# RWKV-7 chunk steps of a decoder trunk: zero-padded whole-array matmuls, another order of outputs and side work

## The chip, the cores and the metric

The kernel runs on one core of one Trainium2 chip. The metric is the device time of one execution in microseconds, the median of several runs. The profile comes from one further execution of the same program.

## The reference, cut to what matters

The program computes two layers of a hybrid trunk for 256 tokens of 1024 channels in float32: a gated mixer of three branches (RG-LRU, gated DeltaNet, RWKV-7), then a PEER expert layer. The change lies in the phase that computes the RWKV branch and, beside it, the input projections of other branches ("side" projections). The recurrence of that branch is, for 16 heads of 64 channels:

```python
def step(state, inp):
    r_t, w_t, k_t, v_t, kk_t, kka_t = inp
    s_kk = einsum('bhvk,bhk->bhv', state, kk_t)
    state = state * w_t[:, :, None, :] - s_kk[..., None] * kka_t[:, :, None, :] + v_t[..., None] * k_t[:, :, None, :]
    return state, einsum('bhvk,bhk->bhv', state, r_t)
...
o = (o - mean) * rsqrt(var + eps)            # group norm over the 64 channels of a head
o = o * lnx_w + lnx_b
o = (o + bonus) * gate
```

## The kernel before

**Phase and loop.** `rwkv_phase` runs once per layer. It walks over eight channel tiles of 128 channels (two heads each): seven in a hardware loop (`more=True`) and the last one outside it (`more=False`). Each engine has its own body: `pe_body` (TensorE), `act_body` (ScalarE), `vec_body` (VectorE), `pool_body` (GpSimd). The engines run their own lists in order and meet at semaphores: `te.wait_ge(V.sem, V.at("S0", i))` waits until VectorE has passed the point labelled "S0" of tile i. The order of the work is written by hand; nothing plans it.

**One tile.** The 256 tokens are four chunks of 64. q counts the chunks; b = q // 2 is the block of 128 tokens, hf = q % 2 the half of the 128 partitions in which the chunk's tokens lie. A tile's work is:
- transposes (`bkT`, `vT`) of NBt, KH and the value, then the small products `g0`, `g1` (L915) that give the masked matrices G1, G2 within a chunk;
- T0 (L926), AV and `bonus` (L937, L940);
- the inversion of 64x64 unit triangular matrices in five levels (`invert64_pe`, L495) into TT;
- the four chunk steps, below;
- the group norm on VectorE (L1217 to L1231), the output transpose `yT` (L982), and y (L1233 to L1237).

**A chunk step before.** St is the 128x128 state of the two heads. R (L955) is the product of the chunk's keys with St, 64 output rows; VectorE adds AVO to it (L1188). U (L963) multiplies by TT; ScalarE copies it to Um (L1070). L968 adds the queries' product with St into the output bank b3. L973 and L974 are the state's increment from the value Vt and from Um, over the 64 rows of the chunk; VectorE masks it (t1, L1201) and updates St (L1204, or L1206 for q = 0), for which SP = decayed St was made at L1190. L976 adds the output's part within the chunk (`O`), and VectorE adds bank b3 to O (L1209).

**Side work.** While TensorE waits in this chain it works on other products: `pe_piece` is part of the projection of r, k, v of the next tile (12 parts, in the inversion's `fill`), and `pe_side` parts of the five side projections f0 to f4 (20 parts). These use split float32: a weight tile and x are each a high part (rounded) and a rest, so a single k (128 of the 1024 inputs) is three matmuls of 128x128 by 256 columns (L332 to L334, L808 to L810). A part is two k. The high parts of the weights are made on ScalarE (`act_round`, L315, L829), the rests on VectorE (`vec_rest`, L320) for r, k, v, f2, f3, f4, and on GpSimd (L834) for f0 and f1. `act_side` copies a finished side projection out. `turn` (L291) is a matmul of the identity whose result nobody reads.

**What VectorE does for the next tile.** `vec_sums`, `vec_roots` (two half reciprocals, L768), `vec_keys` (L772 to L777), `vec_ends` (KH and the chunk ends, L780, L781), `vec_queries` (L785, L786), `vec_bonus` (L763) and `vec_piece` (L871) stand between the steps' own operations. `pe_sums` (L723) is the matmul that sums squares.

**Loads.** SyncE issues the weight tiles in the order r, k, v, `rwkv_up`, f0 to f4 of each tile, each behind the release of its slot in the ring.

Of the kernel before, what the change touches and what calls it, by code (L numbers as in the profile page):

```python
# [99 lines left out]
def _program(nc, ctx, A, out, book):  # L100
# [199 lines left out]
    class Split:  # L300
# [25 lines left out]
        def project(self, te, ps, n, parity, part, x_parts=x_parts):  # L326
            if part % 2 == 0:
                te.wait_ge(self.low, 2 * n + part // 2 + 1)
            for k in range(2 * part, 2 * part + 2):
                w_hi, w_lo = (f32r(w_parts[:, x, parity, k * P:(k + 1) * P]) for x in range(2))  # L330
                x_hi, x_lo = (f32r(x_parts[:, x, k]) for x in range(2))
                te.matmul(ps, w_hi, x_hi, start=(k == 0), stop=False)  # L332
                te.matmul(ps, w_hi, x_lo, start=False, stop=False)  # L333
                mm = te.matmul(ps, w_lo, x_hi, start=False, stop=(k == KT - 1))  # L334
            if part % 2:
                mm.then_inc(self.used, 1)
# [260 lines left out]
    def rwkv_phase(l):  # L597
# [20 lines left out]
        side_rounded, side_rest = lsem("rw_side_rounded"), lsem("rw_side_rest")  # L618

# [20 lines left out]
        Vt = r_(NB, P)  # L640
# [4 lines left out]
        Rs, Um, St, SP, t1 = r_(P), r_(P), r_(P), r_(P), r_(P)  # L645
# [11 lines left out]
        O4 = O.rearrange("p b (h c) -> p (b h) c", h=2)  # L657

# [3 lines left out]
        with nc.Block() as block:  # L662
# [107 lines left out]
            def vec_keys(v, i):  # L770
                v.wait_ge(VA.sem, VA.now(i))
                v.tensor_tensor(kk, kkr, rs, ALU.mult).then_inc(VA.sem, VA.one())  # L772
                v.wait_ge(VA.sem, VA.now(i))
                v.scalar_tensor_tensor(nb, kk, -1.0, aa, ALU.mult, ALU.mult).then_inc(VA.sem, VA.one())
                v.wait_ge(VA.sem, VA.now(i))
                v.wait_ge(SA.sem, SA.at("Pi", i))
                v.tensor_tensor(NBt, nb, Pi, ALU.mult).then_inc(VA.sem, VA.one())  # L777
# [10 lines left out]
            def pe_side(te, i, js, more):  # L788
                for j in js:
                    n, part = divmod(j, 4)  # L790
                    if part == 0:
# [10 lines left out]
                    if n < 2:  # L802
                        if part % 2 == 0:
                            te.wait_ge(side_rest, 4 * i + 2 * n + part // 2 + 1)
                        for k in range(2 * part, 2 * part + 2):
                            w_hi, w_lo = f32r(side_high[:, n, k * P:(k + 1) * P]), f32r(side_low[:, n, k * P:(k + 1) * P])
                            x_hi, x_lo = (f32r(x_parts[:, x, k]) for x in range(2))
                            te.matmul(f_bank[n], w_hi, x_hi, start=(k == 0), stop=False)  # L808
                            te.matmul(f_bank[n], w_hi, x_lo, start=False, stop=False)
                            mm = te.matmul(f_bank[n], w_lo, x_hi, start=False, stop=(k == KT - 1))  # L810
                        if part == 3:
                            mm.then_inc(EF.sem, EF.one(f"f{n}"))
                    else:
                        W.project(te, f_bank[n], tile(f"f{n}", i), parity(f"f{n}"), part)
# [60 lines left out]
            def pe_body(te, i, more):  # L875
                def fill(lev, y):
# [3 lines left out]
                    if more and (lev, y) == (5, 0):  # L880
                        pe_sums(te, i + 1)
                    if more:
                        pe_piece(te, i + 1, 2 * lev + y)
                    elif lev and (y == 0 or lev == 5):
                        if lev == 1:
                            te.wait_ge(SF.sem, SF.at("f0", i))
                        turn(te, ps_in[0], 2)

                def side(*js):
                    pe_side(te, i, js, more)  # L890

# [5 lines left out]
                side(0)  # L897
                te.wait_ge(VA.sem, VA.at("KH", i))
                for x, src in enumerate((NBt, KH)):
                    for b in range(NB):  # L900
                        mm = te.transpose(b5[:, (2 * x + b) * P:(2 * x + b + 1) * P], src[:, b * P:(b + 1) * P], ident)
                mm.then_inc(E.sem, E.one("bkT"))
# [1808 lines left out]
```

## Time and profile before

| | us |
|---|---|
| median of 3 runs | 3372.75 |
| lowest, highest | 3370.45, 3377.39 |
| span of the profiled execution, and its own time | 3373.3 |
| busy: TensorE, VectorE, ScalarE, GpSimd | 3242.0, 2293.5, 1747.5, 251.9 |
| first RWKV phase, last tile's y ends | 455.3 |
| second RWKV phase, last tile's y ends | 2131.2 |

The profiled execution's first to last instruction is its span; nothing beyond the span is recorded. A row of a timeline gives the start in us, the time in us, the engine, the line, the operation, output <- inputs and the count; in brackets stands the engine's idle time just before it and what released it. "issue" there is a wait for nothing that the profile shows. TensorE's matmuls are pipelined, so the busy time of one (some 0.28 us) is longer than the distance to the next start; distances between starts are what matters. An fp32 matmul appears as two records, so "x4" for such lines is two matmuls; transposes and the split products (fp32r) appear as one.

### The profile page before, as it was taken

The numbers are of one execution on the slowest core, as the hardware profiler recorded it, in microseconds if no ns is written. First come the engines' busy times: TensorE is split into PE (matmuls) and PEld (weight loads), VectorE is DVE, ScalarE is ACT, GpSimd is POOL, SyncE is SP. The second block draws the span as 40 slices with busy tenths as digits, with TensorE's granted clock in tenths as the row PEclk, the third lists the DMA queues.
The fourth block names the chain that finished last, engine by engine and source line by source line (L and its number), as shares of the span: only waits on it lengthen the run. The fifth ranks groups of instructions, "written<-read, shape, count | busy, mean of one in ns | idle before, by whom it ended". The sixth has DMA issues, their size and how long they took to land. (4 is left out here: it accounts for less than half of the span.)

```text
span 3373.3 us, 74285 instructions
## 1 busy us (share of the span) xinstructions
PE 3242.0 (96%) x24946; PEld 2825.3 (84%) x24946; DVE 2293.5 (68%) x5014; ACT 1747.5 (52%) x3657; POOL 251.9 (7%) x238
## 2 busy tenths in 40 slices
PE   8999999999999999999989999999999999999998
PEld 7878788889998788888778778888898978888886
DVE  5666666655886677777666665666558866777776
ACT  5555454433296555555555554544323965555554
POOL 2212101100000000000022111021000000000000
PEclk9999999999999999999999999999999999999999
DMA  3222322223323555555432222232242245555553
GB/s 135 91 80 74 112 73 101 92 81 145 106 81 131 187 187 188 191 190 190 158 114 70 96 70 104 76 106 81 82 177 86 75 146 188 189 187 187 190 190 130
DMA packets 122236, 433.34 MB, mean 128 GB/s; under 512 B 15744, under 2 KB 18048, under 8 KB 121344
## 3 DMA queue, kind: packets, MB, share of 16 engines
q1 hardware_dynamic: 122112, 431.74, 36.1%
q8 instruction: 71, 1.16, 0.1%
q14 instruction: 53, 0.43, 0.0%
HBM read 430.64 MB, written 1.05 MB: 128 GB/s over the span
## 5 line engine op out<-in xcount | busy, mean ns | idle before, releaser
L2360 PE MATMUL bank<-x_both,u_parts 128*128 128x512 f32 x1536 | 557.8, 397 | 1.8 <-DVE u_parts L2480 1.8
L2344 PE MATMUL bank<-v_parts,act_high 128*128 128x512 f32 x1024 | 405.0, 396 | 5.9 <-DVE v_parts L2485 4.7
L2346 PE MATMUL bank<-v_parts,act_low 128*128 128x512 f32 x1024 | 399.9, 391 | 0.0
L2356 PE MATMUL bank<-x_both,u_parts 128*128 128x256 f32 x1536 | 399.5, 281 | 0.0
L2345 PE MATMUL bank<-v_parts,act_high 128*128 128x512 f32 x1024 | 398.8, 389 | 0.0
L332 PE MATMUL bank<-x_parts,w_parts 128*128 128x256 f32 x1248 | 394.4, 316 | 1.5 <-DVE w_parts L320 1.5
L2480 DVE TENSOR_TENSOR u_parts<-u_raw,u_parts 128x512 fp32r<-128x512 f32 x384 | 265.5, 692 | 191.7 <-ACT u_parts L2415 191.6
L333 PE MATMUL bank<-x_parts,w_parts 128*128 128x256 f32 x1248 | 352.6, 283 | 0.0
L334 PE MATMUL bank<-x_parts,w_parts 128*128 128x256 f32 x1248 | 351.7, 282 | 0.0
L2485 DVE TENSOR_TENSOR v_parts<-v_raw,v_parts 128x512 fp32r<-128x512 f32 x512 | 329.7, 685 | 31.6 <-ACT v_parts L2422 28.3
L2360 PEld LDWEIGHTS bank<-x_both,u_parts 128*128 128x128 f32 x1536 | 288.5, 188 | 62.5 <-issue 2.6
L2415 ACT ACTIVATE u_parts<-u_raw 128x512 fp32r<-128x512 f32 x384 | 242.5, 632 | 187.5 <-PE bank L2360 147.3
L2422 ACT ACTIVATE v_parts<-v_raw 128x512 fp32r<-128x512 f32 x512 | 292.1, 618 | 27.4 <-DMA v_raw<-in_v 22.7
L2356 PEld LDWEIGHTS bank<-x_both,u_parts 128*128 128x128 f32 x1536 | 289.7, 189 | 16.3
L320 DVE TENSOR_TENSOR w_parts<-ring,w_parts 128x512 fp32r<-128x512 f32 x344 | 254.3, 776 | 27.3 <-ACT w_parts L315 26.5
L332 PEld LDWEIGHTS bank<-x_parts,w_parts 128*128 128x128 f32 x1248 | 237.1, 190 | 40.0 <-issue 19.6
L333 PEld LDWEIGHTS bank<-x_parts,w_parts 128*128 128x128 f32 x1248 | 238.4, 191 | 0.9
L334 PEld LDWEIGHTS bank<-x_parts,w_parts 128*128 128x128 f32 x1248 | 238.1, 191 | 0.0
L2344 PEld LDWEIGHTS bank<-v_parts,act_high 128*128 128x128 f32 x1024 | 193.0, 188 | 52.6 <-DVE v_parts L2485 16.5
L2453 ACT ACTIVATE slots<-slots 128x256 f32<-128x256 f32 x192 | 80.7, 420 | 296.0 <-DVE slots L2531 296.0
L2346 PEld LDWEIGHTS bank<-v_parts,act_low 128*128 128x128 f32 x1024 | 192.2, 188 | 43.3
L2345 PEld LDWEIGHTS bank<-v_parts,act_high 128*128 128x128 f32 x1024 | 192.4, 188 | 39.8
(374 smaller groups left out, 6334.4 us busy)
## 6 DMA issues: line engine op xcount, KB each, us to landing
v_raw<-in_v SPq DMA_DIRECT2D x256, 512.0 KB, 3.5
u_raw<-in_u SPq DMA_DIRECT2D x192, 512.0 KB, 4.5
ring<-in_w_side SPq DMA_DIRECT2D x80, 512.0 KB, 3.5
ring<-in_w_gdn SPq DMA_DIRECT2D x64, 512.0 KB, 3.5
ring<-in_w_rwkv SPq DMA_DIRECT2D x48, 512.0 KB, 6.1
ring<-in_w_gdn_side SPq DMA_DIRECT2D x32, 512.0 KB, 3.5
ring<-in_u SPq DMA_DIRECT2D x32, 512.0 KB, 3.6
u_ring<-in_u SPq DMA_DIRECT2D x32, 512.0 KB, 3.5
```

The costliest lines, as they stand in the source:

```text
L320: v.tensor_tensor(f32r(w_parts[:, 1, parity, self.cols(half)]), raw[:, self.cols(half)], w_parts[:, 0, parity, self.cols(half)], ALU.subtr ...
L332: te.matmul(ps, w_hi, x_hi, start=(k == 0), stop=False)
L333: te.matmul(ps, w_hi, x_lo, start=False, stop=False)
L334: mm = te.matmul(ps, w_lo, x_hi, start=False, stop=(k == KT - 1))
L2344: te.matmul(ps, f32r(w_hi), f32r(x_hi), start=start, stop=False, **kw)
L2345: te.matmul(ps, f32r(w_hi), f32r(x_lo), start=False, stop=False, **kw)
L2346: return te.matmul(ps, f32r(w_lo), f32r(x_hi), start=False, stop=stop, **kw)
L2356: return te.matmul(banks[r % 4][:, T:2 * T], f32r(u_lo[:, cols]), f32r(xhigh[:, k]), start=False, stop=stop)
L2360: mm = te.matmul(banks[r % 4][:, :].rearrange("p (x t) -> p x t", x=2), f32r(u_hi[:, cols]), f32r(x_both[:, :, k]), start=(k == 0), stop=( ...
L2422: a_.activation(f32r(v_hi[r % 2][:, half(n)]), v_raw[:, r % 2, half(n)], ACT.Copy).then_inc(v_high, 1)
L2480: v.tensor_tensor(f32r(u_lo[:, half(n)]), u_raw[:, r % 2, half(n)], u_hi[:, half(n)], ALU.subtract).then_inc(u_low, 1)
L2485: v.tensor_tensor(f32r(v_lo[r % 2][:, half(n)]), v_raw[:, r % 2, half(n)], v_hi[r % 2][:, half(n)], ALU.subtract)\
```

## The change

- **Whole array.** Vt becomes VX, with two copies for the chunk halves, each zero in the other half's 64 rows; Um becomes UX likewise. The zeros are written once per phase on GpSimd. With them the state's increment runs over all 128 rows, R and the queries' product fill all 128 output rows, and only U and the reads within the chunk (`reads`) stay 64x64.
- **Outputs beside the next step's U.** The queries' product follows R at once; the reads of step q-1 stand behind U of step q. The outputs alternate between two banks (OB = b3, b4). ScalarE's copy of U no longer waits for O. VectorE's output add of step q-1 (`out_add`) stands behind the R-add of step q and side pieces.
- **Side projections by single k.** The 20 parts become 40 k: 2 and 14 ahead of T0, then 1 behind R, 1 behind U, 2 behind the state's increment, and the rest at the end.
- **Order on VectorE.** SP is made behind the state update; f3's rest goes from q=1 to q=2, f4's stays in q=3, behind an output add; `vec_roots`, `vec_bonus`, `vec_piece`, the keys, KH and the queries move as the diff shows.
- **Others.** `pe_sums` goes behind the piece of its level; the side copy of f3 goes behind the root on ScalarE; `idle` puts two turns before a wait in the last tile.
- The prologue (tile 0) calls the same VectorE functions, with the first root half ahead of the last shift.

```diff
-Vt = r_(NB, P)
+VX = r_(2, NB, P)
...
-Rs, Um, St, SP, t1 = r_(P), r_(P), r_(P), r_(P), r_(P)
+Rs, St, SP, t1 = r_(P), r_(P), r_(P), r_(P)
+UX = r_(2, P)
...
+OB = (b3, b4)
...
-def vec_keys(v, i):
+def vec_key(v, i):
...
+def vec_beta(v, i):
...
+def vec_betas(v, i):
...
-    v.tensor_tensor(NBt, nb, Pi, ALU.mult).then_inc(VA.sem, VA.one())
+    v.tensor_tensor(NBt, nb, Pi, ALU.mult).then_inc(VA.sem, VA.one("NBt"))
...
-        if part == 3:
+        if k == KT - 1:
-        W.project(te, f_bank[n], tile(f"f{n}", i), parity(f"f{n}"), part)
+        W.project_k(te, f_bank[n], tile(f"f{n}", i), parity(f"f{n}"), k)
...
         pe_gates(te, i + 1)
-    if more and (lev, y) == (5, 0):
-        pe_sums(te, i + 1)
     if more:
...
         turn(te, ps_in[0], 2)
+    if more and (lev, y) == (5, 0):
+        pe_sums(te, i + 1)
...
+def idle(n):
+    if not more:
+        turn(te, b6, n)
...
 rows = lambda q: slice(64 * q, 64 * q + 64)
-side(0)
-te.wait_ge(VA.sem, VA.at("KH", i))
-for x, src in enumerate((NBt, KH)):
-    for b in range(NB):
-        mm = te.transpose(b5[:, (2 * x + b) * P:(2 * x + b + 1) * P], src[:, b * P:(b + 1) * P], ident)
-mm.then_inc(E.sem, E.one("bkT"))
+te.wait_ge(VA.sem, VA.at("NBt", i))
+for b in range(NB):
+    te.transpose(b5[:, b * P:(b + 1) * P], NBt[:, b * P:(b + 1) * P], ident)
 for b in range(NB):
...
 te.matmul(b6[:, T:2 * T], small[:, P:2 * P], SG, start=True, stop=True).then_inc(E.sem, E.one("gate"))
+te.wait_ge(VA.sem, VA.at("KH", i))
+for b in range(NB):
+    mm = te.transpose(b5[:, (2 + b) * P:(3 + b) * P], KH[:, b * P:(b + 1) * P], ident)
+mm.then_inc(E.sem, E.one("bkT"))
+side(0, 1)
...
-side(1, 2, 3, 4)
+side(*range(2, 16))
...
-                               G2[rows(hf), 2 * hh + b, x], Vt[rows(hf), b, hh * HD:(hh + 1) * HD], start=True, stop=True)
+                               G2[rows(hf), 2 * hh + b, x], VX[rows(hf), hf, b, hh * HD:(hh + 1) * HD], start=True, stop=True)
...
+def reads(q):
+    b, hf = divmod(q, 2)
+    for hh in range(2):
+        mm = te.matmul(OB[hf][rows(hf), hh * HD:(hh + 1) * HD], G1[rows(hf), 2 * hh + b, 1], UX[rows(hf), hf, hh * HD:(hh + 1) * HD],
+                       start=(q == 0), stop=True, skip_group_check=True)
+    mm.then_inc(E.sem, E.one(f"O{q}"))
+left = list(range(16, 40))
+step_side = lambda n: side(*(left.pop(0) for _ in range(n)))
 for q in range(T // CH):
...
     if q:
-        if not more:
-            turn(te, b4, 1)
+        idle(2)
         te.wait_ge(V.sem, V.at(f"S{q - 1}", i))
...
             te.wait_ge(SA.sem, SA.at("a", i + 1))
-        te.matmul(b5[rows(hf), 0:P], KR[:, b, 0, rows(hf)], St, start=True, stop=True).then_inc(E.sem, E.one(f"R{q}"))
-        side(2 * q + 7)
-        if not more:
-            turn(te, b4, 1)
+        te.matmul(b5[:, 0:P], KR[:, b, 0], St, start=True, stop=True).then_inc(E.sem, E.one(f"R{q}"))
+        if q > 1:
+            te.wait_ge(V.sem, V.at(f"o{q - 2}", i))
+        te.matmul(OB[hf][:, 0:P], KR[:, b, 1], St, start=True, stop=False, skip_group_check=True)
+        step_side(1)
         te.wait_ge(V.sem, V.at(f"R{q}", i))
...
     if q:
-        te.wait_ge(V.sem, V.at(f"o{q - 1}", i))
-        te.matmul(b3[rows(hf), 0:P], KR[:, b, 1, rows(hf)], St, start=True, stop=False)
-    side(2 * q + 8)
+        reads(q - 1)
+    if q < 3:
+        te.matmul(b2[:, 0:P], BK[:, 2 + b], VX[:, hf, b], start=True, stop=False)
+    step_side(1)
     te.wait_ge(S.sem, S.at(f"U{q}", i))
-    te.sem_inc(passed, 1)
     if q < 3:
-        te.matmul(b2[:, 0:P], BK[rows(hf), 2 + b], Vt[rows(hf), b], start=True, stop=False)
-        te.matmul(b2[:, 0:P], BK[rows(hf), b], Um[rows(hf)], start=False, stop=True).then_inc(E.sem, E.one(f"S{q}"))
-    for hh in range(2):
-        mm = te.matmul(b3[rows(hf), hh * HD:(hh + 1) * HD], G1[rows(hf), 2 * hh + b, 1], Um[rows(hf), hh * HD:(hh + 1) * HD],
-                       start=(q == 0), stop=(hh == 1) or q == 0)
-    mm.then_inc(E.sem, E.one(f"O{q}"))
-side(15, 16, 17, 18, 19)
+        te.matmul(b2[:, 0:P], BK[:, b], UX[:, hf], start=False, stop=True).then_inc(E.sem, E.one(f"S{q}"))
+        step_side(2)
+    else:
+        te.sem_inc(passed, 1)
+        reads(q)
+side(*left)
 te.wait_ge(V.sem, V.at("on", i))
...
-a.activation(Vt, vps, ACT.Copy).then_inc(S.sem, S.one("Vt"))
+for hf, rows in enumerate(halves):
+    a.activation(VX[rows, hf], vps[rows], ACT.Copy).then_inc(S.sem, S.one(f"V{hf}"))
...
     a.wait_ge(E.sem, E.at(f"U{q}", i))
-    if q:
-        a.wait_ge(E.sem, E.at(f"O{q - 1}", i))
     rows = halves[q % 2]
-    a.activation(Um[rows], b7[rows, 0:P], ACT.Copy).then_inc(S.sem, S.one(f"U{q}"))
+    a.activation(UX[rows, q % 2], b7[rows, 0:P], ACT.Copy).then_inc(S.sem, S.one(f"U{q}"))
     if q == 0 and more:
...
         act_round(a, i, "f4")
-act_side(a, i, 3)
...
 a.activation(va4, va4, ACT.Sqrt).then_inc(S.sem, S.one("sd"))
+act_side(a, i, 3)
 a.wait_ge(SF.sem, SF.at("f2", i))
...
         vec_sums(v, i + 1)
+    if n == 2 and not more:
+        W.skip(v, W.low, tile("r", NI), 3)
     if n == 5:
-        if not more:
-            W.skip(v, W.low, tile("r", NI), 3)
         vec_rest(v, i, "f2")
     if more and n == 5:
-        vec_bonus(v, i + 1)
+        vec_roots(v, i + 1, 0)
...
+def out_add(q):
+    b, hf = divmod(q, 2)
+    rows = halves[hf]
+    v.wait_ge(E.sem, E.at(f"O{q}", i))
+    v.wait_ge(S.sem, S.at("AVO", i))
+    v.tensor_tensor(O[rows, b], O[rows, b], OB[hf][rows, 0:P], ALU.add).then_inc(V.sem, V.one(f"o{q}"))
...
         v.tensor_tensor(Rs[rows], b5[rows, 0:P], AVO[rows, b], ALU.add).then_inc(V.sem, V.one(f"R{q}"))
-        if q < 3:
-            v.tensor_scalar(SP, St, end, None, ALU.mult).then_inc(V.sem, V.one())
-        if q != 2:
-            vec_rest(v, i, {1: "f3", 3: "f4"}[q])
-        if q < 3 and more:
-            vec_roots(v, i + 1, q - 1)
+        if q == 1 and more:
+            vec_piece(v, i + 1, 2)
+            vec_bonus(v, i + 1)
+        if q == 2:
+            vec_rest(v, i, "f3")
         if q == 2 and more:
-            vec_keys(v, i + 1)
+            vec_roots(v, i + 1, 1)
         if q == 3 and more:
-            vec_ends(v, i + 1)
+            vec_key(v, i + 1)
+            vec_beta(v, i + 1)
+        out_add(q - 1)
+        if q == 3:
+            vec_rest(v, i, "f4")
     if q < 3:
...
-    v.wait_ge(E.sem, E.at(f"O{q}", i))
-    v.wait_ge(S.sem, S.at("AVO", i))
-    v.tensor_tensor(O[rows, b], O[rows, b], b3[rows, 0:P], ALU.add).then_inc(V.sem, V.one(f"o{q}"))
-    if q == 0 and more:
-        vec_piece(v, i + 1, 2)
...
-if more:
-    vec_queries(v, i + 1)
+        if q < 2:
+            v.wait_ge(V.sem, V.now(i))
+            v.tensor_scalar(SP, St, ends[:, q + 1:q + 2], None, ALU.mult).then_inc(V.sem, V.one())
+out_add(3)
...
 v.tensor_scalar(va4, va4, 1.0 / HD, GN_EPS, ALU.mult, ALU.add).then_inc(V.sem, V.one("var"))
+if more:
+    vec_betas(v, i + 1)
 v.wait_ge(S.sem, S.at("sd", i))
...
 v.tensor_tensor(O4, O4, bc(va4), ALU.mult).then_inc(V.sem, V.one("on"))
+if more:
+    vec_ends(v, i + 1)
+    vec_queries(v, i + 1)
 v.wait_ge(E.sem, E.at("yT", i))
...
+norm.all_ready(g)
+for n, x in enumerate((VX, UX)):
+    for hf in range(2):
+        if n + hf:
+            g.wait_ge(zeros, 2 * n + hf)
+        g.memset(x[halves[1 - hf], hf], 0.0).then_inc(zeros, 1)
+g.wait_ge(zeros, 4)
```

## Rows read from the trace of the kernel before

**Rows 1.** The page, busy time, share and instructions per engine.
```profile
PE 3242.0 (96%) x24946; PEld 2825.3 (84%) x24946; DVE 2293.5 (68%) x5014; ACT 1747.5 (52%) x3657; POOL 251.9 (7%) x238
```
**Rows 2.** TensorE's timeline, three output transposes; then a windows row (PEclk is the clock).
```profile
148.10 0.44 PE L982 MATMUL bank<-made_of_shapes,arena 128*128 128x128 f32 x2 [1.36 <-DVE arena L1231]
...
199.84 0.44 PE L982 MATMUL bank<-made_of_shapes,arena 128*128 128x128 f32 x2 [1.35 <-DVE arena L1231]
...
253.23 0.44 PE L982 MATMUL bank<-made_of_shapes,arena 128*128 128x128 f32 x2 [1.36 <-DVE arena L1231]
...
202.00:203.00 1.00, 1.00 (x6) 0.85 (x4) 0.13 (x1) 0.99 (x2) 0.00 (x0) 0.50 0.03 12
```
**Rows 3.** Waits of TensorE, 98 to 409 us: total, times, longest.
```profile
PE bank L955 <- DVE arena L1204: 4.8, 12, 0.4
PE bank L723 <- DVE arena L756: 4.2, 6, 0.7
```
**Rows 4.** TensorE's timeline, U of q=0, then the step q=2.
```profile
179.88 0.44 PE L963 MATMUL bank<-arena 64*64 64x64 f32 x4
...
186.96 0.43 PE L955 MATMUL bank<-arena 128*64 128x128 f32 x2 [0.40 <-DVE arena L1204]
187.32 0.39 PE L332 MATMUL bank<-x_parts,w_parts 128*128 128x256 f32 x1
...
188.23 0.44 PE L963 MATMUL bank<-arena 64*64 64x64 f32 x4
188.60 0.43 PE L968 MATMUL bank<-arena 128*64 128x128 f32 x2
...
189.87 0.49 PE L973 MATMUL bank<-arena 64*128 64x128 f32 x2
...
191.35 0.43 PE L955 MATMUL bank<-arena 128*64 128x128 f32 x2 [0.40 <-DVE arena L1204]
```
**Rows 5.** TensorE's timeline in the last tile: a side matmul, then turns.
```profile
447.10 0.28 PE L334 MATMUL bank<-x_parts,w_parts 128*128 128x256 f32 x1
447.22 0.38 PE L291 MATMUL bank<-made_of_shapes 128*128 128x128 f32 x2
...
453.64 1.28 PE L291 MATMUL bank<-made_of_shapes 128*128 128x128 f32 x10
```
**Rows 6.** VectorE's timeline in the steps.
```profile
184.88 0.95 DVE L768 RECIPROCAL arena<-arena 128x128 f32<-128x128 f32 x1
...
187.43 0.28 DVE L1188 TENSOR_TENSOR arena<-bank,arena 64x128 f32<-64x128 f32 x1 [0.20 <-PE bank L955]
...
190.61 0.29 DVE L1201 TENSOR_TENSOR arena<-bank,made_of_shapes 128x128 f32<-128x128 f32 x1 [0.38 <-PE bank L974]
190.94 0.35 DVE L1204 SCALAR_TENSOR_TENSOR arena<-arena 128x128 f32<-128x128 f32 x1
...
192.14 1.29 DVE L320 TENSOR_TENSOR w_parts<-ring,w_parts 128x512 fp32r<-128x512 f32 x2
```
**Rows 7.** ScalarE's timeline, the copy of U.
```profile
188.78 0.27 ACT L1070 ACTIVATE arena<-bank 64x128 f32<-64x128 f32 x1 [4.12 <-PE bank L963]
```
**Rows 8.** VectorE's timeline in the tail.
```profile
194.73 0.29 DVE L1209 TENSOR_TENSOR arena<-arena,bank 64x128 f32<-64x128 f32 x1 [0.88 <-PE bank L976]
195.06 0.43 DVE L785 TENSOR_TENSOR arena<-arena 128x256 f32<-128x256 f32 x1
...
199.15 0.18 DVE L1229 RECIPROCAL arena<-arena 128x4 f32<-128x4 f32 x1 [1.22 <-ACT arena L1082]
```
**Rows 9.** SyncE's issues of r, k, v; their landings; ScalarE ahead of the r round.
```profile
194.71 1.57 SPq L584 DMA_DIRECT2D ring<-in_w_rwkv  x3
...
DMA to landing us min/median/max: 4.8/6.1/6.7
...
201.23 1.28 ACT L315 ACT_TABLE_LOAD   x1
```
**Rows 10.** GpSimd's timeline in the first prologue.
```profile
25.14 3.04 POOL L834 TENSOR_TENSOR side_low<-ring,side_high 128x512 fp32r<-128x512 f32 x2 [3.83 <-ACT side_high L829]
```

More of the change, by code:

```diff
@@ L326, in project, with project_k @@
         def project(self, te, ps, n, parity, part, x_parts=x_parts):
-            if part % 2 == 0:
-                te.wait_ge(self.low, 2 * n + part // 2 + 1)
             for k in range(2 * part, 2 * part + 2):
[L330 to L335, printed above, removed]
+                self.project_k(te, ps, n, parity, k, x_parts)
+        def project_k(self, te, ps, n, parity, k, x_parts=x_parts):
+            if k % (KT // 2) == 0:
+                te.wait_ge(self.low, 2 * n + k // (KT // 2) + 1)
+            w_hi, w_lo = (f32r(w_parts[:, x, parity, k * P:(k + 1) * P]) for x in range(2))
+            x_hi, x_lo = (f32r(x_parts[:, x, k]) for x in range(2))
+            te.matmul(ps, w_hi, x_hi, start=(k == 0), stop=False)
+            te.matmul(ps, w_hi, x_lo, start=False, stop=False)
+            mm = te.matmul(ps, w_lo, x_hi, start=False, stop=(k == KT - 1))
+            if k % (KT // 2) == KT // 2 - 1:
                 mm.then_inc(self.used, 1)
@@ L618, in rwkv_phase @@
         side_rounded, side_rest = lsem("rw_side_rounded"), lsem("rw_side_rest")
+        zeros = lsem("rw_zeros")
         number = {"r": 0, "k": 1, "v": 2, "f2": 9, "f3": 10, "f4": 11}
@@ L789, in pe_side @@
                 for j in js:
-                    n, part = divmod(j, 4)
-                    if part == 0:
+                    n, k = divmod(j, KT)
+                    if k == 0:
                         if n == 0:
@@ L802, in pe_side @@
                     if n < 2:
[L803 to L810, printed above, removed]
-                        if part == 3:
+                        if k % (KT // 2) == 0:
+                            te.wait_ge(side_rest, 4 * i + 2 * n + k // (KT // 2) + 1)
+                        w_hi, w_lo = f32r(side_high[:, n, k * P:(k + 1) * P]), f32r(side_low[:, n, k * P:(k + 1) * P])
+                        x_hi, x_lo = (f32r(x_parts[:, x, k]) for x in range(2))
+                        te.matmul(f_bank[n], w_hi, x_hi, start=(k == 0), stop=False)
+                        te.matmul(f_bank[n], w_hi, x_lo, start=False, stop=False)
+                        mm = te.matmul(f_bank[n], w_lo, x_hi, start=False, stop=(k == KT - 1))
+                        if k == KT - 1:
                             mm.then_inc(EF.sem, EF.one(f"f{n}"))
                     else:
-                        W.project(te, f_bank[n], tile(f"f{n}", i), parity(f"f{n}"), part)
+                        W.project_k(te, f_bank[n], tile(f"f{n}", i), parity(f"f{n}"), k)
             def act_round(a, i, *whats, halves=(0, 1)):
@@ L927, in pe_body @@
                 mm.then_inc(E.sem, E.one("T0"))
-                side(5, 6, 7)
                 te.wait_ge(S.sem, S.at("gate", i))
@@ L1015, in _ @@
                 W.skip(te, W.used, 3, 3, W.PRIME)
+                te.wait_ge(zeros, 4)
                 EA.end()
@@ L1276, in _ @@
                 vec_sums(v, 0)
+                vec_roots(v, 0, 0)
+                vec_piece(v, 0, 2)
                 vec_bonus(v, 0)
-                vec_piece(v, 0, 2)
-                for half in range(2):
-                    vec_roots(v, 0, half)
-                vec_keys(v, 0)
+                vec_roots(v, 0, 1)
+                vec_key(v, 0)
+                vec_beta(v, 0)
+                vec_betas(v, 0)
                 vec_ends(v, 0)
```

## The prediction

> **What bounds the kernel now.** I read the page's busy shares first: TensorE is busy 3242.0 of 3373.3 us, VectorE 68% [rows 1]. So only what shortens TensorE's own sequence, or its few gaps, moves the end. The printed chain of waits covers just the last 17 us, so I went by TensorE's timeline in the phase that the diff touches. That phase runs 16 times (8 channel tiles, two layers), 14 of them in the loop form (`more`) and two as the last tile. From one output transpose (L982) to the next is 51.74 us (148.10 to 199.84), once 53.39 (199.84 to 253.23) [rows 2]. The table of waits over six iterations shows TensorE idle before L955 (twelve times 0.40) and before L723 (six times 0.70) [rows 3]; before L982 it is 1.36 each time [rows 2]. With a third, shorter wait at L955 that is some 3.2 us of an iteration, the rest is streaming. A gain above that must come out of the matmuls' own spacing.
>
> Rows 4 show one chunk step on TensorE, R2 (the L955 of q=2) at 186.96 to R3 at 191.35: 4.39 us. R takes 0.36 to the next start, a side part of six matmuls 0.91, U 0.37, L968 0.36, again 0.91 with its edges, the two L973/L974 0.32 each, the reads 0.44, then 0.40 idle. Side matmuls in a run start 0.12 apart [rows 5], so six are 0.71 and entering and leaving them costs 0.2.
>
> **What a change of shape costs.** The edge behind a side group costs 0.1 where a 64-row block follows, but in rows 5 the full 128x128 turn L291 starts 0.12 behind the side matmul before it (447.10 to 447.22), which is the side matmuls' own spacing; and the U behind this turn comes 0.32 later, where a turn inside a run of five costs (1.28-0.27)/4.5 = 0.225. So leaving 128x128 costs about 0.1, and staying costs nothing. The old step changes the array's shape seven times (128x64, 128x128, 64x64, 128x64, 128x128, 64x128, 64x64, 128x64); the new one goes to 64x64 for U and the reads and back: twice.
> The Trainium skill says the same in "TensorEngine Tiling (Array Packing)", Key Properties: changing the tiling mode drains the engine. It gives no price. The same page speaks against the change too: with contract dimensions of 64, row tiling gives up to twice the throughput. By that rule the zero-padded whole-array matmuls would waste half; here the blocks concerned stand alone and the old K=64 pair has 0.32 per matmul [rows 4], so the trace bears out the first rule and not the second.
>
> **The steps, new.** I price a whole-array fp32 matmul of 128 columns at 0.225 [rows 5]. Its upper end is what the part-array forms cost now, 0.32 to 0.36 [rows 4]; its lower end is not below 0.2, since the same number of columns streams. A single k is three matmuls, 0.36; entry from fp32 0.1; each change of shape 0.1 to 0.15.
> - R to U: R 0.225 plus 0.1 of start-up where it waited, output half (L968's work moved here) 0.225, entry 0.1, one k 0.36, change 0.1: 1.07. The wait hidden: VectorE starts the R-add 0.47 behind R and needs 0.28 [rows 4, 6], so U could start at 0.82. Covered. (Before: 1.27.)
> - U to the second S matmul: U and the reads of the step before, eight 64x64 records: four cost 0.37 with 0.16 of edge, so eight 0.58; change 0.1; the V matmul 0.225; entry 0.1; one k 0.36: about 1.35. The U copy on ScalarE ends 0.82 behind U [rows 4, 7]: covered, also now that it no longer waits for O. (Before: 1.96.)
> - Second S matmul to the next R: the tail is VectorE's. From L974 (0.32 behind L973, so 190.19) to t1 0.42, t1 and the state update end 1.10, R at 1.16 [rows 4, 6]. TensorE's work there is 0.225 + 0.1 + two k 0.71 = 1.04, so about 0.1 idle is left of the 0.40.
> The step from R1 to R2 is 3.6 (was 4.39). R2 to R3 is set by VectorE: behind the R-add (to 0.75) stand the f3 rest, two halves 1.21, half a reciprocal 0.95, the out-add 0.27, then t1 and the state update 0.68 [rows 6]: 3.85. For q=1 the same place holds a shift and the bonus, 1.0, which fit. q=0: U, V matmul, k, S, two k are 2.2 of TensorE, but a half reciprocal now stands before t1: R1 at 2.4 (was 2.69, from U0 at 179.88 to R1, which is 4.39 before R2).
> SP (the decayed state) moves behind the state update: 0.3 us in VectorE's wait for R. Covered.
>
> **The tail.** R3 to the transpose: before 8.49 (191.35 to 199.84), 1.35 of it idle. New for TensorE: 1.07 + 0.58 + 0.1 + k 0.46 + change 0.1 + last reads 0.37 + eleven k 4.05 = 6.75. New for VectorE: R-add 0.75, two key products to 1.65, out-add 2 to 1.9, f4 rest to 3.1, then out-add 3 at 3.1. From out-add 3 (194.73) to the transpose (199.84) was 5.11 [rows 2, 8], of which some 0.7 was the two queries from 195.06 on (they move behind the transpose's release) and 1.22 the wait for the root, held by a table load for side tile 3. That side copy now stands behind the root; in the gap stands one product, 0.45. This leaves 3.7, so the transpose starts at 6.85: a tie, 0.1 idle. If the f4 rest were before out-add 2 nothing would change; it is what sets this end.
>
> **Inversion.** `pe_sums` goes behind a piece: the 0.70 idle before L723 [rows 3] is covered by a piece of 0.9; with its start-up 0.8.
> **Start of the body.** One part of two k moved behind the transposes of NBt, and T0 and AV are now neighbours: a group edge less, 0.15. KH, ends and the queries now run behind L1231 on VectorE (1.25 us) before y; the g matmuls wait for y0, due at 1.8 behind the transpose, while TensorE gets there at 2.8. Covered by 1 us; if that goes, it costs what is late.
> **Queues.** The f4 rest ends 3.1 behind R3 instead of 2.0. The SP queue has its slot's reload next, and behind it r, k and v: they were issued at 194.71 [rows 9], 3.36 behind R3; new 4.5. The first of them took 4.8 to land, and ScalarE's r round begins behind the table load of 201.23, at 202.5, 11.2 behind R3 [rows 9]; new it lands at 9.3 and is wanted 1.4 earlier, at 9.8. Slack falls from 3 us to 0.5; a miss of 1 us would still lie inside VectorE's 3 us of lead before T0. VX as two copies adds 0.3 to ScalarE, which has a table load less (1.28). The four memsets are on GpSimd in the prologue: it idles 3.83 us before L834 there [rows 10], and two 128x512 tensor ops take 3.04 there, so four memsets of at most 64x256 fit. The prologue's PE no longer waits for KH but for NBt one product earlier, and does its side part later: nothing. So these edits are priced at nothing, -0.5 to +1 us per layer.
>
> **Sum, full iteration.** Steps and tail 19.96 to 2.4 + 3.6 + 3.85 + 6.85 = 16.7: 3.26. With inversion 0.8 and start 0.15: 4.2. Fourteen: 59. In the last tile `idle(2)` puts two turns before each wait, as before in sum but now side by side (0.45 instead of twice 0.3 with their edges); its step was 3.99 of work and 0.6 of turns, 4.6, and becomes 1.07 + 1.35 + 1.04 + 0.45 = 3.9. With q=0 and a tail bound by about the same 3.7 behind out-add 3, 2.5 per layer: 5.
>
> **The clock.** In the windows row at 202 the granted clock is 0.50, that is 1.2 GHz instead of 2.4 [rows 2]. It fell right behind a stretch in which TensorE stood 1.35 and 0.30 idle around the transpose, and that iteration took 1.65 us longer. Five of the 14 intervals have such a fall. With some 0.4 idle left there I expect four of five gone: 6.5; ends 0 and 8 (or new falls: -3).
> Total 59 + 5 + 6.5 = 71. The profiled execution is 3373.3, the median 3372.75, half a microsecond apart: I forecast 3302.
>
> **Rivals.**
> 1. Shape changes are not what costs; spacing is by matmul. Every whole-array matmul keeps the slot of its part-array form (0.32 to 0.36), and the third group edge per step adds 0.2. Then the step is 0.34+0.36+0.55+0.37+0.37+0.36+0.55+0.36+0.91 = 4.17, q=0 2.54, the tail 7.2: 2.1 saved instead of 3.26; the last tile nothing. 14 x 2.9 = 41, with the clock 3327. For it: 0.36 stands in rows 4 for both L955 and L968. Against: rows 5. 24%.
> 2. VectorE's order: three pieces now stand between R-add and t1 or out-add 3. If each of these is late by another 0.5 to 1 us per iteration (f4's operands late, or ScalarE's table load behind U3 later than the variance), half of the gain goes: 3340. Against: VectorE was idle before every L1201. 9%.
> 3. Slower: a whole-array fp32 matmul with 128-row weights and full outputs costs double or more, 0.7. Twelve per iteration, 192 in all, at 0.47 above my price are 90 us against a gain of 71: 3392. It decides from 0.37 us above my price. Against: the L291 run at 0.225. 3%.
> 4. The change leaves TensorE's end where it was, because ring loads (slack 0.5 us) stop ScalarE's r round for several us: 3372. 2%.
>
> **How the numbers follow.** Forecast 62%, own range 3290 to 3316 (price of a matmul 0.2 to 0.27, clock gain -3 to 8). Rivals 24, 9, 3, 2. The range 3288 to 3334 takes in the first rival. A difference of 0.2% (6.7 us) is what a measurement can tell: faster 0.94, same 0.02, slower 0.04.
>
> **What would show it.** R1 to R2 near 3.6 and R2 to R3 near 3.85 (t1 released by VectorE's own queue); no idle before L723; idle before the transpose under 0.4; out-add 3 starting 3.1 behind R3; 47.5 us per iteration; fewer stretches at half clock; starts behind a side k at 0.12 where the next is whole-array. Steps of 4.2 with no idle show rival 1; VectorE gaps before t1 that end in ScalarE rival 2; starts 0.5 apart at the new matmuls rival 3.

## The result and the profile after

The changed kernel takes 3284.11 us in the median (3282.35 to 3287.17), the kernel before, run beside it, 3371.6 us: a ratio of 0.9743 with a 95% interval of 0.9729 to 0.9757. That is 87.5 us less. I had forecast 3302, with a range down to 3288, so the direction and the order of size were right and the gain was still larger than my range allowed. In the profiled executions the span fell from 3373.3 to 3281.8 us, by 91.5.

The page of the changed kernel, busy time, share and instructions of each engine (before: [rows 1]):
```profile
PE 3181.3 (97%) x24946; PEld 2796.3 (85%) x24946; DVE 2291.9 (70%) x5014; ACT 1716.0 (52%) x3645; POOL 253.7 (8%) x246
```
TensorE does as many instructions as before in 61 us less of busy time. So only a third of the gain is idle time removed. The rest lies in how close together the matmuls stand and, for some 7 to 8 us of it, in the clock (below).

TensorE's timeline of the changed kernel: U0, then the step R1 to R2 (L978 is R, L981 the queries' product, L987 U, L965 the reads, L993 the V matmul, L997 the S matmul, L335 to L337 a side k). It answers to [rows 4]. A step runs from one R to the next:
```profile
168.54 0.44 PE L987 MATMUL bank<-arena 64*64 64x64 f32 x4
...
170.77 0.49 PE L978 MATMUL bank<-arena 128*128 128x128 f32 x2
171.09 0.39 PE L981 MATMUL bank<-arena 128*128 128x128 f32 x2
171.24 0.36 PE L335 MATMUL bank<-x_parts,w_parts 128*128 128x256 f32 x1
...
171.76 0.27 PE L987 MATMUL bank<-arena 64*64 64x64 f32 x1
171.78 0.27 PE L965 MATMUL bank<-arena 64*64 64x64 f32 x1
171.87 0.22 PE L987 MATMUL bank<-arena 64*64 64x64 f32 x1
171.88 0.22 PE L965 MATMUL bank<-arena 64*64 64x64 f32 x1
...
172.15 0.49 PE L993 MATMUL bank<-arena 128*128 128x128 f32 x2
172.39 0.36 PE L335 MATMUL bank<-x_parts,w_parts 128*128 128x256 f32 x1
...
172.84 0.39 PE L997 MATMUL bank<-arena 128*128 128x128 f32 x2
172.98 0.36 PE L335 MATMUL bank<-x_parts,w_parts 128*128 128x256 f32 x1
173.18 0.28 PE L336 MATMUL bank<-x_parts,w_parts 128*128 128x256 f32 x1
...
173.99 0.49 PE L978 MATMUL bank<-arena 128*128 128x128 f32 x2
```
R1 to R2 is 173.99 - 170.77 = 3.22 us; a step was 4.39. Read the starts: the records of U and of the reads alternate, 0.01 apart, and the V matmul starts 0.39 behind U, where U alone took 0.37 before (188.23 to 188.60 in [rows 4]). The trace of the kernel before held this already, in L937. Its 32 records of 64x64 go to two opposite corners of the array in turn and take 1.08 in all, 0.03 each, while the records of U, all on one corner, follow each other at 0.06:
```profile
157.84 1.15 PE L937 MATMUL bank<-arena 64*64 64x64 f32 x32
158.92 0.70 PE L940 MATMUL bank<-arena,made_of_shapes 128*128 128x256 f32 x2
```

TensorE's waits in the changed kernel, 92 to 380 us (total, times, longest), against [rows 3]:
```profile
PE bank L978 <- DVE arena L1237: 4.8, 6, 0.8
PE bank L1005 <- DVE arena L1263: 2.0, 6, 0.3
```
Both old entries are gone, L723's by the move and L955's by the fuller step. What is left is one wait of 0.80 per iteration ahead of R3 and 0.34 ahead of the output transpose. VectorE's timeline shows what holds R3:
```profile
174.52 0.28 DVE L1218 TENSOR_TENSOR arena<-bank,arena 64x128 f32<-64x128 f32 x1 [0.26 <-PE bank L978]
174.73 1.27 DVE L320 TENSOR_TENSOR w_parts<-ring,w_parts 128x512 fp32r<-128x512 f32 x2
175.93 0.94 DVE L774 RECIPROCAL arena<-arena 128x128 f32<-128x128 f32 x1
176.90 0.29 DVE L1210 TENSOR_TENSOR arena<-arena,bank 64x128 f32<-64x128 f32 x1
177.22 0.29 DVE L1234 TENSOR_TENSOR arena<-bank,made_of_shapes 128x128 f32<-128x128 f32 x1
177.54 0.35 DVE L1237 SCALAR_TENSOR_TENSOR arena<-arena 128x128 f32<-128x128 f32 x1
```
There is no gap between the R-add (L1218) and t1 (L1234): f3's rest, the half reciprocal and the output add (L1210) fill it, as forecast. The tail is the stretch from R3 to the output transpose. TensorE again, its two ends ([rows 2, 4]):
```profile
177.95 0.49 PE L978 MATMUL bank<-arena 128*128 128x128 f32 x2 [0.80 <-DVE arena L1237]
...
184.81 0.44 PE L1005 MATMUL bank<-made_of_shapes,arena 128*128 128x128 f32 x2 [0.34 <-DVE arena L1263]
```

The distances between these marks are the same in every iteration, to some hundredths; only the start of the body is longer where the clock falls (12.8 us before), and once by 0.2 us after. In us:

| loop iteration | before | forecast | after |
|---|---|---|---|
| transpose to the first piece (start of the body) | 11.17 | 11.0 | 10.58 |
| first piece to U0 (inversion) | 20.6 | 19.8 | 19.9 |
| U0 to R1 | 2.69 | 2.4 | 2.23 |
| R1 to R2 | 4.39 | 3.6 | 3.22 |
| R2 to R3 | 4.39 | 3.85 | 3.96 |
| R3 to the transpose | 8.49 | 6.85 | 6.86 |
| iteration, clock at full speed | 51.75 | 47.5 | 46.75 |
| last tile, transpose to transpose | 43.16 | 40.7 | 38.80 |

The clock. These windows rows cover the two loops of each kernel, from their first transpose to that of the last tile (PEclk, the granted clock, is the third number from the end), before first:
```profile
96.44:453.50 357.06, 335.49 (x3949) 286.06 (x3950) 230.15 (x513) 186.04 (x355) 66.74 (x59) 0.99 0.25 85
1770.80:2129.40 358.60, 336.97 (x3949) 287.21 (x3950) 230.27 (x513) 186.10 (x355) 66.72 (x59) 0.99 0.25 85
```
```profile
91.30:410.80 319.50, 311.09 (x3948) 275.88 (x3948) 229.76 (x517) 172.91 (x350) 66.69 (x59) 1.00 0.29 98
1722.60:2041.80 319.20, 310.82 (x3948) 275.71 (x3948) 229.79 (x517) 172.89 (x350) 66.69 (x59) 1.00 0.29 98
```
The five stretches of 3.4 us at 1.2 GHz are gone; both loops now run at 2.4 GHz throughout.

### The profile page after: what moved, and what is told of

Same layout as the page of the kernel before. It is cut to its first block and busy times, and to the rows that moved or that the text cites. A ratio compares the mean times of both kernels' runs of the same rounds, so it can differ in the third digit from the quotient of the medians.

```text
span 3281.8 us, 74221 instructions
## 1 busy us (share of the span) xinstructions
PE 3181.3 (97%) x24946; PEld 2796.3 (85%) x24946; DVE 2291.9 (70%) x5014; ACT 1716.0 (52%) x3645; POOL 253.7 (8%) x246
## 5 line engine op out<-in xcount | busy, mean ns | idle before, releaser
L335 PE MATMUL bank<-x_parts,w_parts 128*128 128x256 f32 x1248 | 394.7, 316 | 1.1 <-DVE w_parts L320 1.1
L337 PE MATMUL bank<-x_parts,w_parts 128*128 128x256 f32 x1248 | 351.7, 282 | 0.0
L335 PEld LDWEIGHTS bank<-x_parts,w_parts 128*128 128x128 f32 x1248 | 237.5, 190 | 23.7 <-issue 5.3
L337 PEld LDWEIGHTS bank<-x_parts,w_parts 128*128 128x128 f32 x1248 | 237.5, 190 | 0.0
```

## The experiments

Each ratio is against the kernel before on the same chip. Steps are read from TensorE's timelines as above. Experiments 2, 4, 5, 6 and 8 were executed once each and have no ratio: they are read by their timelines alone, in which each mark repeats from iteration to iteration to some hundredths.

**1. The new order with part-array matmuls** (`e1_rows_all`).
```diff
-te.matmul(b5[:, 0:P], KR[:, b, 0], St, ...)
+te.matmul(b5[rows(hf), 0:P], KR[:, b, 0, rows(hf)], St, ...)
...
-te.matmul(b2[:, 0:P], BK[:, b], UX[:, hf], ...)
+te.matmul(b2[:, 0:P], BK[rows(hf), b], UX[rows(hf), hf], ...)
```
The queries' product and the V matmul were changed alike.

> The changed kernel with its order kept, but R, the queries' product, the V matmul and the S matmul back on part of the array (64 output rows, or 64 contraction rows). Theory (shape changes cost about 0.1 each, order gives the rest): R1 to R2 goes from 3.22 to about 3.5, U0 to R1 from 2.23 to 2.4, R2 to R3 stays 3.96 and the tail 6.86 (both set by VectorE), so about 0.5 us per iteration and 8 us in all, 3292. Rival (every matmul keeps its old slot of 0.32 to 0.36): step 4.2, at least 2 us per iteration, 3315 or more. Rival (the form of the matmuls does nothing, all is order): 3284 and 3.22.

Measured: ratio 0.9815 (0.9799 to 0.9832), against 0.9743 for the whole array. R1 to R2 is 3.79, U0 to R1 2.66, R2 to R3 3.90, tail 6.80, iteration 47.65. TensorE's timeline of it:
```profile
171.89 0.49 PE L997 MATMUL bank<-arena 64*128 64x128 f32 x2
172.31 0.39 PE L335 MATMUL bank<-x_parts,w_parts 128*128 128x256 f32 x1
...
173.21 0.43 PE L978 MATMUL bank<-arena 128*64 128x128 f32 x2
```
Behind the 64-row S matmul the side k starts after 0.42; behind the whole-array one it was 0.14 (172.84 to 172.98). And R comes 1.32 behind S, because TensorE now fills the time and VectorE, at 1.15, is no longer the last. So the form of four small matmuls is worth 0.57 us in this step, more than the 0.3 that I gave for it here, and the order alone is worth 0.60. Both rivals fall, but my own number was too small as well: the form is worth 0.9 us per iteration, not 0.5, and 2.7 in each last tile (which takes 41.48 here instead of 38.80). The order and the other edits alone bring 62 of the 87 us (0.9815). What this does not separate is the change of shape from the form itself: in the kernel before, L973 takes 0.32 to L974, which has the same shape, where the whole-array S takes 0.14. No run has part-array matmuls in a longer row of their own shape, so the price per change of shape stays an argument.

**2. Only R and the queries' product on 64 rows** (`e2_rows_r`): the first pair of the diff above.

> The changed kernel with only R and the queries' product on 64 output rows again; V and S matmuls stay whole. Of the 0.57 that the step R1 to R2 lost with all four (3.22 to 3.79) this has the pair 128x64 with one change of shape more ahead of the side k: theory 0.2, step 3.4; the other 0.35 then belongs to V and S. Rival (each of the four costs the same): 3.5.

Measured: R1 to R2 3.35, so 0.13 for this pair and the other 0.44 for V and S. But R2 to R3 and the tail each shrank by 0.06: VectorE's R-add starts 0.47 behind this R of 64 output rows and 0.53 behind the whole-array one, and VectorE sets both stretches. So the iteration is 46.75 as in the changed kernel, and the pair on the whole array wins nothing in the loop. It wins 0.95 in each last tile (38.80 instead of 39.75), where TensorE sets the steps. "Each costs the same" is refuted; my 3.4 was 0.05 too high.

**3. The whole array in the old order** (`e7_whole_in_before`): the kernel before with VX and UX, their memsets, and the four matmuls of experiment 1 on all 128 rows.

> The kernel before with its order, but R, the queries' product, V and S matmuls on the whole array with zero halves. Theory (shape): R to U 1.27 to 1.15, U to the second S matmul 1.96 to 1.65, its latency to R 1.16 stays: step 4.39 to 4.0; with q=0 and the tail 1.2 us per iteration, 20 us in all, 3352. Rival (form does nothing): 3372, step 4.39. Rival (whole array costs more): a step above 4.39.

Measured: ratio 0.9949 (0.9932 to 0.9965), steps 4.02 and 3.98, U0 to R1 2.51, tail 8.22: 1.26 us per iteration at full clock. Theory confirmed to 0.05. Alone the form is thus worth 17 of the 87 us (12 to 23 by the interval), and with the 62 of experiment 1 some 8 come only from both together. The wait ahead of R (L957 here) grew from 0.40 to up to 0.50, and that of the sums stayed at 0.70: the old order leaves VectorE's work behind S uncovered. The clock fell in 5 of its 14 intervals between output transposes, as in the kernel before.

**4. U and the reads on the same rows** (`e4_same_half`); the reads beside U then use the zero half and write rows that nobody adds, so this output lacks three of the four reads.
```diff
-reads(q - 1)
+reads(q - 1, hf)      # rows of q, as U
```

> The changed kernel with the reads of step q-1 that stand behind U of step q put on the same 64 rows as U (they then read the zero half and write rows that nobody adds: the output lacks these parts). Theory (U and the reads of the other half run at the same time, which is why the pair takes 0.39 and not the 0.58 that I priced): U to the V matmul becomes about 0.6 and R1 to R2 3.4. Rival (the second group is cheap because it needs no change of shape): 0.39 and 3.22 stay.

Measured: R1 to R2 3.44. TensorE's timeline:
```profile
172.29 0.44 PE L988 MATMUL bank<-arena 64*64 64x64 f32 x4
172.57 0.39 PE L966 MATMUL bank<-arena 64*64 64x64 f32 x4
172.90 0.49 PE L994 MATMUL bank<-arena 128*128 128x128 f32 x2
```
Now the records stand one group behind the other and U to the V matmul is 0.61 instead of 0.39. With the same matmuls on opposite corners of the array they had started in pairs. This is shown: 0.22 us per step come from two groups at once. The Trainium skill has it in "TensorEngine Tiling (Array Packing)", Key Properties: different tiles can execute weight loads and matmuls in parallel. By that rule I should have priced the pair at one group; the trace agrees, with 0.39 for the pair and 0.37 for U alone.

**5. The sums ahead of the piece again** (`e5_sums_back`).
```diff
+if more and (lev, y) == (5, 0):
+    pe_sums(te, i + 1)
 if more:
     pe_piece(te, i + 1, 2 * lev + y)
```

> The changed kernel with the matmul that sums squares back ahead of the piece of its level. Theory: its idle of 0.70 comes back and T0 to U0 goes from 21.79 to 22.55, 10 us in all. Rival (VectorE's sums come back earlier with it and the state update of q=0 gains): under 0.3 per iteration.

Measured: 0.71 more from T0 to U0 in every iteration (22.50 for 21.79), the wait is back, all other marks unmoved:
```profile
PE bank L729 <- DVE arena L762: 4.2, 6, 0.7
```

**6. The side copy of f3 ahead of the root again** (`e6_side3_back`): `act_side(a, i, 3)` back above the root.

> The changed kernel with the side copy of f3 on ScalarE back ahead of the root (a table load of 1.28 between). Theory (the table load is what held the root; moving it made the tail): the root comes late again, R3 to transpose from 6.86 to 7.5 or more, idle before the transpose 0.34 to 1 us, and some stretches of half clock come back in the loops: 10 to 20 us more. Rival (the table load fits ahead of the variance, since VectorE's f4 rest now delays it): tail stays 6.86, no stretch.

Measured: tail 7.88 (1.02 more), iteration 47.76. ScalarE's timeline, TensorE's waits, then TensorE around one output transpose:
```profile
183.61 1.28 ACT L857 ACT_TABLE_LOAD   x1 [2.02 <-PE bank L337]
184.91 0.47 ACT L857 ACTIVATE zg<-bank,arena 128x256 f32 x1
185.40 1.28 ACT L1103 ACT_TABLE_LOAD   x1
```
```profile
PE bank L1005 <- DVE arena L1263: 9.5, 7, 1.4
```
```profile
187.72 0.44 PE L1005 MATMUL bank<-made_of_shapes,arena 128*128 128x128 f32 x2 [1.36 <-DVE arena L1263]
188.20 0.43 PE L912 MATMUL bank<-made_of_shapes,arena 128*128 128x128 f32 x2
```
The two table loads hold the root, as thought. But the clock did not fall: with 1.36 us of idle before every transpose, as in the kernel before, both loops took 325.38 us and show full clock, the first in this row:
```profile
92.20:417.50 325.30, 310.78 (x3948) 275.69 (x3948) 231.02 (x517) 188.50 (x362) 66.72 (x59) 1.00 0.28 95
```
So that idle alone does not bring the falls, in this one profile of 14 intervals; this half of my theory failed. What differs from the kernel before is the time behind the transpose: in this run the next matmul starts 0.48 behind it, with 0.05 idle; in the kernel before a second idle of 0.25 to 0.30 stands there:
```profile
200.58 0.38 PE L808 MATMUL bank<-x_parts,side_high 128*128 128x256 f32 x1 [0.30 <-issue]
```
Whether that is the cause was not tested by itself.

**7. Turns ahead of the transpose in the kernel before** (`e12_turns_before`, again as `e15_turns_again`; `e14_before_again` is the kernel before on that second chip).
```diff
+if more:
+    turn(te, b2, 5)
 te.wait_ge(V.sem, V.at("on", i))
```

> The kernel before with five turns of the identity ahead of the wait for the output transpose in the loop form: TensorE is as late for it, but busy. Theory (the clock falls there because TensorE stands idle): no stretch of 0.50 in the two RWKV loops (before: five), every iteration 51.75 to 51.8, 8 us less, 3356 to 3364. Rival (the falls belong to something else at this place): five stay. Rival (the turns are late themselves and hold the transpose): every iteration longer by up to 0.2.

> The kernel before with five turns ahead of the output transpose, again. Theory: no stretch of 0.50 in the loops, and 5 to 8 us less than before in the times too. Rival (the earlier result of the times, 1 us): the half-clock stretches gone from the loops come back elsewhere, ratio 0.9985 to 1.

> The kernel before, unaltered, profiled on another chip. Theory (the falls of the clock at the output transpose belong to the kernel): 4 to 6 stretches of 0.50 in the two RWKV loops again, each 1.65 us. Rival (they belong to the one profiled execution): other numbers, none to two.

Measured: ratios 0.9993 (0.9984 to 1.0003) and 0.9972 (0.996 to 0.9983). Windows rows of the first loop, the kernel before again, then the second run with turns:
```profile
97.90:454.90 357.00, 335.22 (x3947) 285.89 (x3948) 230.21 (x514) 186.01 (x355) 66.73 (x59) 0.99 0.26 85
```
```profile
96.30:449.90 353.60, 338.86 (x4009) 290.10 (x4009) 230.02 (x513) 186.16 (x355) 66.69 (x59) 1.00 0.26 86
```
The kernel before has four falls in its loops this time, with turns there is none in either run, and every iteration is 51.7 to 51.8. Turns take 3.4 us off each loop (357.0 to 353.6), two falls of 1.65. In the medians this came to 1 us once and 8 us once, and the two intervals do not overlap. The phases outside the loops had 36 us at half clock in the first profile and 26 in the second, a difference as large as the effect that I looked for. The clock term of the change is thus 7 to 8 us in a profile; its worth in the median I can only put between 1 and 8.

**8. Pairs of side k** (`e9_pairs`): two behind R, none behind U for q > 0, two behind S.

> The changed kernel with two side k behind R, none behind U for q>0 and two behind S (same total). Theory: R to U grows by one k (0.36) and U to S shrinks only to ScalarE's 0.88 from 1.08, so R1 to R2 is 3.4 instead of 3.22; R2 to R3 stays 3.96 or 4.0. Rival (an edge of a side group costs 0.2 and one less pays): 3.2 or less.

Measured: R1 to R2 3.41, R2 to R3 4.08, tail 6.98. The theory holds for the first (3.4); R2 to R3 and the tail grew by 0.12 each, which I had not expected. Single k pay 0.43 us per iteration. New waits for the U copy (L965, 0.4) and for the weights' rests (L335, 0.4) appear:
```profile
PE bank L965 <- ACT arena L1093: 2.6, 6, 0.4
PE bank L335 <- DVE w_parts L320: 2.3, 6, 0.4
```

**9. The roots early** (`e8_roots_early`, again as `e8b_roots_early`).
```diff
 if q == 1 and more:
     vec_piece(v, i + 1, 2)
-    vec_bonus(v, i + 1)
+    vec_roots(v, i + 1, 1)
...
-if q == 2 and more:
-    vec_roots(v, i + 1, 1)
...
     vec_ends(v, i + 1)
+    vec_bonus(v, i + 1)
     vec_queries(v, i + 1)
```

> The changed kernel with the second half reciprocal moved from q=2 to q=1 on VectorE and the bonus product moved from q=1 to behind KH. Theory (R2 to R3 is 3.96 instead of 3.22 only because of VectorE's queue ahead of t1): R2 to R3 falls to 3.25, R1 to R2 stays 3.22 to 3.3, tail unchanged at 6.86, so 0.7 us in each of 14 iterations, 10 us, 3274. Rival (something else holds the update of q=2, such as the f3 rest or TensorE): under 0.2 us per iteration, 3282 to 3284.

> The version with the roots early again, on the same chip as the run beside it: 0.972 of before, 46.0 us per iteration.

Measured: ratios 0.9718 (0.9702 to 0.9735) and 0.9709 (0.9695 to 0.9722), 3270 and 3272 us. The theory holds: R2 to R3 is 3.22, iteration 46.01, the wait ahead of R is gone, and VectorE has a gap before t1 of q=1 again:
```profile
169.80 0.94 DVE L774 RECIPROCAL arena<-arena 128x128 f32<-128x128 f32 x1
170.66 0.22 DVE L1210 TENSOR_TENSOR arena<-arena,bank 64x128 f32<-64x128 f32 x1
171.03 0.29 DVE L1232 TENSOR_TENSOR arena<-bank,made_of_shapes 128x128 f32<-128x128 f32 x1 [0.16 <-PE bank L997]
```

**10. Levelling VectorE's list** (`e10_balanced`, `e13_shift_behind`). On top of 9, half of f2's rest goes into the wait for the sums, `vec_key` from q=3 to q=1, and the last shift to q=0: ahead of t1 in the first kernel, behind SP in the second. `e11_after_again` is the changed kernel beside the first.

> The version with the roots early, and VectorE's list levelled further: half of the f2 rest into its wait for the sums, the last shift ahead of t1 of q=0, the first key product from q=3 to q=1. Theory (the tail is VectorE's, idle 0.34 before the transpose): R3 to transpose 6.86 to 6.6, the steps stay 3.22, 4 us less than with the roots early alone (0.972 of before to 0.971). Rival (the pieces ahead of t1 in q=0 and q=1 make these updates late): U0 to R1 or R1 to R2 longer by 0.1 to 0.3, nothing gained.

> The levelled version with the last shift of q=0 behind the state update instead of ahead of t1. Theory (the levelled version lost 0.25 in U0 to R1 only by this place): U0 to R1 back from 2.48 to 2.23, R3 to transpose stays 6.62, steps 3.22; 45.8 us per iteration, 3 us less than the version with the roots early. Rival (the shift behind the update delays the R-add): R1 to R2 3.4.

> The changed kernel unaltered, for its ratio on the same chip as the run beside it: 0.974 of before, R2 to R3 3.96.

Measured: ratios 0.972 (0.9706 to 0.9733) and 0.9709 (0.9695 to 0.9723); the changed kernel 0.9743 (0.973 to 0.9757). Both have the tail at 6.62, as expected. The first pays with U0 to R1 at 2.48 (2.23), the second with R1 to R2 at 3.40 (3.23), so an iteration is 46.02 and 45.87 against 46.01. The 3 to 4 us that I expected from each over experiment 9 do not show in the times. VectorE's timeline of the second:
```profile
168.92 0.48 DVE L880 SCALAR_TENSOR_TENSOR arena<-bank,arena 128x255 f32<-128x255 f32 x1
169.44 0.29 DVE L1221 TENSOR_TENSOR arena<-bank,arena 64x128 f32<-64x128 f32 x1
169.76 0.95 DVE L774 RECIPROCAL arena<-arena 128x128 f32<-128x128 f32 x1
170.75 0.42 DVE L778 TENSOR_TENSOR arena<-arena 128x256 f32<-128x256 f32 x1
```
R1 was at 168.74; the R-add (L1221) starts 0.70 behind it, because the shift (L880) runs into its time, where it starts 0.53 behind R in the changed kernel. The rival came true, and what one gap gives the other takes. The best version is thus 9 (or the last one, equal in its times), at 0.971.

## Why the prediction was off

**Most of the mechanism held.** The waits ahead of L955 and L723, the whole-array form, the late root and the f3 and f4 rests all acted where I had put them. The S matmul to R came to 1.15 (forecast 1.16) and the sums' move to 0.71 (0.8). The wait for R3 is VectorE's (forecast 3.85, measured 3.96: I left out 0.1 of gaps between its instructions). Experiments 5, 6 and 9 show these one by one. That the tail came to 6.86 (forecast 6.85) is partly luck: output add 3 started 3.29 behind R3 instead of 3.1, and the rest took 3.57 instead of 3.7.

**The step that failed is the price of "U to the second S matmul"**: I wrote "four cost 0.37 with 0.16 of edge, so eight 0.58", then a change 0.1, V 0.225, entry 0.1, k 0.36, about 1.35. Measured: 1.08. The whole miss lies in the first two terms: U, the reads and the change of shape were priced at 0.68, one group behind the other, and took 0.39 (171.76 to 172.15), since they run at once (experiment 4 shows 0.22 for it). V, entry and k were priced at 0.685 and took 0.69 (172.15 to 172.84).

**A smaller miss is the "entry 0.1" from a whole-array fp32 matmul into a side group.** Behind V, which comes out of the 64x64 group, it is there. Behind the queries' product and S it is not: S to its side k is 0.14, and 0.22 with the 0.08 by which the first side matmul takes longer than the others (0.20 to the next start, 172.98 to 173.18, against 0.12). That is the 0.225 that I gave for the matmul alone. I had taken the edge of 0.2 around a side group in rows 4 for one between fp32 and the split products; experiment 1 shows that most of it belongs to the part-array form (0.42 against 0.14). So R to U took 0.99; I had written 1.07, and its terms add up to 1.11.

Together this is nearly all of the 0.38 in R1 to R2 (0.28 and 0.08). U0 to R1 has no reads to pair; there 0.17 were missed, the entries among them. In R2 to R3 VectorE hides it.

**The start of the body** was put at 0.15 and gave 0.59, as large a miss as the steps. The 0.30 of "issue" ahead of the first side matmul had no place in my sum; with whole-array transposes first in the loop it shrank to 0.05: the next matmul starts 0.49 behind the transpose instead of 0.69 to 0.74. The side group behind the KH transposes costs no entry either, and T0 takes 0.52 to AV instead of 0.61 to a side group. These were not tested one by one.

**The last tile** gained 4.36 per layer and not 2.5. I had reckoned TensorE-bound steps of 3.9, with the pair and the entries priced as above; they are 3.35.

The sum, from the profiles: 14 iterations at 5.0 instead of 4.2 give 11.5 us more, the last tiles 3.7, the falls of the clock in the loops 8.2 instead of 6.5. The remaining 4 us lie behind the last RWKV loop, 1243.9 to 1240.0 us, where nothing was changed and where the stretches at half clock were 6 us shorter. The profiles of the experiments scatter there by as much (1239 to 1245), so this last part may be chance.

**Rival 1** (old slots for all) would have given 4.17 and fell with the first timeline. **Rival 2** is in part real: VectorE's order does set R3, at the price I had already put in. **Rival 3** fell: the whole-array matmuls take 0.14 to 0.33 to the next start. **Rival 4** (ring loads) came close. ScalarE's and VectorE's timelines of the changed kernel:
```profile
188.03 1.28 ACT L315 ACT_TABLE_LOAD   x1 [1.57 <-DMA ring<-in_w_rwkv]
```
```profile
189.99 0.69 DVE L320 TENSOR_TENSOR w_parts<-ring,w_parts 128x512 fp32r<-128x512 f32 x1 [2.55 <-ACT w_parts L315]
```
I had left 0.5 us of slack; the load of r is 1.57 late. VectorE's TT0 then ends at 192.68 and TensorE wants it at 193.50: the lead of 3 us is down to 0.8, and nothing is lost yet.

**The clock** was priced by a mechanism, idle time ahead of the transpose, that is only half right: turns there remove the falls (experiment 7), but the same idle in the new order does not bring them (experiment 6). They go with the old order and not with the form of the matmuls: the whole array in the old order had five (experiment 3), the part-array form in the new order none (experiment 1). Which part of the old order it takes besides the idle stays open.

## What to carry to other kernels

Look at the distance from one start to the next across a change of the array's shape before pricing small matmuls: a matmul padded with zeros to 128x128 can be cheaper than its 64-row half when its neighbours use the whole array, and small ones that must stay small should be put next to each other on opposite corners. Look first whether the old trace already holds such a pair: here L937 did. Work for a waiting engine belongs into the longest latency of the chain (here the 1.15 us from the S matmul to R), in pieces small enough to end with it. Once such a chain is filled, the other engine's list decides, so count its instructions between the two points as carefully as those of the engine that was full.

## What the runs showed of the hardware

- A float32 matmul of 64x64 weights by 64 columns in one corner of the array and one in the opposite corner start 0.01 us apart; two such pairs take 0.39 us to the next start. On the same rows the same four matmuls take 0.61.
- Between side matmuls of 128x128 a float32 S matmul takes 0.14 us to the next start on the whole array and 0.42 on 64 rows; the first side matmul behind it takes 0.20 and 0.22 to the next, the others 0.12.
- VectorE's read of R starts 0.53 us behind an R of 128 output rows and 0.47 behind one of 64.
- The granted clock fell to 1.2 GHz in 4 to 5 of 14 intervals of the kernel before, and in 5 of 14 when its matmuls were on the whole array (experiment 3), around an idle of 1.36 us with 0.25 to 0.30 more behind it. It fell in none with turns ahead of the transpose, and in none of the new order with the same 1.36 us and 0.05 behind it.
